# Attention by minima one and two tiles ahead, and small constants turned by TensorE

## The reference

```python
s_loc = jnp.einsum('bjqhd,bkjwhd->bhjqkw', qr, kb).astype(jnp.float32) * scale
s_loc = jnp.where(mask, s_loc + bias.astype(jnp.float32)[None], -jnp.inf)
s_ctx = jnp.einsum('bjqhd,bchd->bhjqc', qr, kc).astype(jnp.float32) * scale
p = jax.nn.softmax(jnp.concatenate([s_loc, s_ctx], axis=-1), axis=-1)
```

## Time and profile before

| | |
|---|---|
| runs | 3012.37 us median of 3 (3010.71 to 3012.51) |
| profiled execution | 3007.67 us, span 3005.7 us |
| busy share of the span | PE 92%, DVE 60%, ACT 41%, POOL 16% |
| start and first group | 0 to 129 us |
| groups 1 to 8 | 129 to 530 us, PE busy 401 of 401 us |
| Fourier phase | 530 to 685 us |
| attention | 685 to 1140 us |
| mixing output, feed-forward | 1140 to 3005 us, PE busy 1758 of 1865 us |

### The profile page before, as it was taken

One profiled execution on the slowest core, in us unless ns is written; L12 is line 12 of the kernel. 1 busy time (PEld: TensorE's weight loads), 2 busy tenths in 40 slices (PEclk: granted clock), 3 DMA queues, 4 the chain that ended last, 5 costly groups with the idle time before them and its releaser, 6 DMA issues. The chain is left out here.

```text
span 3005.7 us, 49988 instructions
## 1 busy us (share of the span) xinstructions
PE 2753.7 (92%) x17010; PEld 2486.7 (83%) x17010; DVE 1788.5 (60%) x3028; ACT 1240.7 (41%) x2612; POOL 466.2 (16%) x670
## 2 busy tenths in 40 slices
PE   4899999766999996998799999999999979999996
PEld 4899999655777785876799999999999968888875
DVE  3533432155999993776777876667666633452445
ACT  2111111125888881322555565556555532122121
POOL 0000000043444330224010000000000000320312
PEclk7999999878999997999899999999999989999998
DMA  8223231498576544463655555544444444334243
GB/s 277 85 85 113 85 95 61 154 361 176 116 146 129 124 80 134 157 203 106 192 167 171 166 192 167 160 153 149 153 151 151 128 154 154 96 129 145 74 129 133
DMA packets 409340, 435.70 MB, mean 145 GB/s; under 512 B 131260, under 2 KB 302286, under 8 KB 406480
## 3 DMA queue, kind: packets, MB, share of 16 engines
q1 hardware_dynamic: 384400, 417.32, 46.5%
q10 hardware_dynamic: 23168, 10.38, 1.2%
q0 software_dynamic: 1600, 5.77, 0.5%
HBM read 311.18 MB, written 124.57 MB: 145 GB/s over the span
## 5 line engine op out<-in xcount | busy, mean ns | idle before, releaser
L2132 PE MATMUL fu_alpha<-fu_h,fu_w 128*128 128x384 f32 x3168 | 574.5, 336 | 19.8 <-DVE fu_h L2358 10.6
L2132 PEld LDWEIGHTS fu_alpha<-fu_h,fu_w 128*128 128x128 f32 x3168 | 553.5, 189 | 22.3 <-issue 22.2
L2618 PE MATMUL fd_acc<-fd_w,fd_f 128*128 128x512 f32 x2376 | 546.5, 392 | 27.4 <-DVE fd_w L2646 18.0
L2618 PEld LDWEIGHTS fd_acc<-fd_w,fd_f 128*128 128x128 f32 x2376 | 447.8, 189 | 126.0 <-issue 18.4
L2132 PE MATMUL fu_beta<-fu_h,fu_w 128*128 128x384 f32 x1584 | 285.4, 334 | 0.6 <-DVE fu_h L2358 0.6
L2132 PEld LDWEIGHTS fu_beta<-fu_h,fu_w 128*128 128x128 f32 x1584 | 275.4, 188 | 1.1 <-issue 1.1
L579 PE MATMUL pj_gps<-pj_ht,w_in 128*128 128x256 f32 x2160 | 270.1, 285 | 0.0
L579 PEld LDWEIGHTS pj_gps<-pj_ht,w_in 128*128 128x128 f32 x2160 | 264.8, 192 | 1.3
L2642 DVE TENSOR_TENSOR fd_f<-fd_f_stage,fd_f 128x512 fp32r<-128x512 f32 (+1 forms) x110 | 91.2, 831 | 284.6 <-ACT fd_f L2598 284.6
L2598 ACT CAST fd_f<-fd_f_stage 128x512 fp32r<-128x512 f32 (+1 forms) x110 | 63.6, 581 | 443.3 <-PE fd_acc L2618 400.8
L2332 DVE TENSOR_TENSOR fu_w<-up_w_stage,fu_w 128x512 fp32r<-128x512 f32 x264 | 181.7, 689 | 84.7 <-ACT fu_w L2196 82.9
(11 more groups left out here) (213 smaller groups left out, 4165.9 us busy)
## 6 DMA issues: line engine op xcount, KB each, us to landing
up_w_stage<-in_w_gu_dram SPq DMA_DIRECT2D x88, 512.0 KB, 4.2
fu_w_sums<-w_gu_sums SPq DMA_DIRECT2D x132, 256.0 KB, 2.9
fd_w_stage<-in_w_down_dram SPq DMA_DIRECT2D x54, 512.0 KB, 3.7
fd_f_stage<-f_t SPq DMA_DIRECT2D x88, 256.0 KB, 2.7
at_k<-k_t SPq DMA_DIRECT2D x28, 704.0 KB, 12.6
w_gu_sums<-fu_w_sums SPq DMA_DIRECT2D x66, 256.0 KB, 5.0
fo_w<-in_w_ada_dram SPq DMA_DIRECT2D x8, 2048.0 KB, 15.0
up_w_stage<-in_w_gu_dram SPq DMA_DIRECT2D x44, 256.0 KB, 4.5
```

The lines of the kernel that those rows point to most:

```text
L2132: mm = pe.matmul(out, w[x][:, j, k, :], b[y][:, j, k, :], start=opens and (k, x, y) == (0, HI, HI), stop=(k, x, y) == (KH - 1, LO, HI), sk ...
L2618: mm = pe.matmul(acc[:, t, at], f[a][:, slot, t * P:(t + 1) * P], w[b][:, w_at(st, slot), at], start=is_step(st, 0) and (a, b) == (HI, HI) ...
```

## The change

In the projection the conditioning vectors, `b_ada` and `a_bs` are loaded as 36 rows of 128 (`small`), turned by one TensorE transpose, and read from PSUM. In group 0 ACT and DVE take the blocks of `w_in` in several pieces between their other work, and `norm_x(2)` comes after the last one. In the attention the queries are scaled by -1/8 and the bias is negated, so a minimum is sought in place of a maximum. The context minimum of a tile is the starting value of the local minimum, which makes the combining instruction needless. Exponentials are taken with scale -1, one tile ahead of the turns; scores and minima are made two tiles ahead, between the turn of the local and of the context part. Row sums have four slots in place of three.

```diff
+        small = zbt[0:ROWS, 0, P:2 * P]
+        turned_small = abps[:, 0, 0:ROWS]
...
-                with nc.allow_non_contiguous_dma(reason="conditioning vectors, channel on partition"):
-                    for v in (LAT, CTX):
-                        sp.dma_start(cond[:, v, :], conds[v].rearrange("(k p) -> p k", p=P)).then_inc(cond_loaded, 16)
+                sp.dma_start(small[COND_ROW:BIAS_ROW, :], conds.rearrange("v (k p) -> (v k) p", p=P)).then_inc(small_loaded, 16)
...
-                    if next2:
+                    first_group = isinstance(g, int) and g == 0
+                    if next2 and not first_group:
                         row_rstd(g + 2)
                     gate_rstd(g * NT + 1)
+                    if first_group:
+                        row_rstd(g + 2)
...
+                act.dma_start(small[BIAS_ROW:BS_ROW, :], b_ada[0, 0:2 * D].rearrange("(k p) -> k p", p=P)).then_inc(small_loaded, 16)
+                act.dma_start(small[BS_ROW:ROWS, :], a_bs.rearrange("l h p -> (l h) p")).then_inc(small_loaded, 16)
                 act.dma_start(zbt[:, 0, 0:P], dft_c64).then_inc(consts_loaded, 16)
                 act.dma_start(zbt[:, 1, 0:P], dft_s64).then_inc(consts_loaded, 16)
                 act.dma_start(ws[:, :, :].rearrange("p a (b q) -> p (a b) q", q=P), a_ws.rearrange("l h p q -> p (l h) q")).then_inc(fw_loaded, 16)
+                act.wait_ge(silu_zeroed, 1)
+                act.wait_ge(small_turned, 1)
+                act.activation(silu[:, :, 0:2].rearrange("p k v -> p v k"),
+                               turned_small[:, COND_ROW:BIAS_ROW].rearrange("p (v k) -> p v k", v=2), ACT.Silu).then_inc(silu_done, 1)
...
                 act.wait_ge(fw_zeroed, 1)
                 for g in range(4):
                     pair, half = g // 2, g % 2
                     act.dma_start(fw2[half * 64:half * 64 + 64, pair * P + half * 64:pair * P + half * 64 + 64],
                                   f_w[0, g]).then_inc(fw_loaded, 16)
-                act.wait_ge(cond_loaded, 32)
-                act.wait_ge(silu_zeroed, 1)
-                act.activation(silu[:, :, 0:2].rearrange("p k v -> p v k"), cond[:, :, :], ACT.Silu).then_inc(silu_done, 1)
-
-                with nc.allow_non_contiguous_dma(reason="biases, channel on partition"):
-                    act.dma_start(mod_bias[:, :], b_ada[0, 0:2 * D].rearrange("(k p) -> p k", p=P)).then_inc(mod_bias_loaded, 16)
-                    act.dma_start(bs[:, :], a_bs.rearrange("l h p -> p (l h)")).then_inc(consts_loaded, 16)
...
                     round_h(0, 0, j)
-                for n in range(3, len(W_BLOCKS)):
-                    high_w(n)
+                high_w(3)
 
                 def group(g, s, next2, next1, is_ctx):
-                    if next1 is not None:
-                        for j in range(SUB):
-                            round_h(g + 1, 1 - s, j, used=g)
                     unit, staged = [0], [0]
+                    first_group = isinstance(g, int) and g == 0
+
+                    def round_next():
+                        if next1 is not None:
+                            for j in range(SUB):
+                                round_h(g + 1, 1 - s, j, used=g)
+
+                    def first_high(*blocks):
+                        if first_group:
+                            for n in blocks:
+                                high_w(n)
+
+                    if not first_group:
+                        round_next()
...
                     gelu(0)
-                    round_qk(HD ** -0.5)
+                    first_high(4)
+                    if first_group:
+                        round_next()
+                    round_qk(-(HD ** -0.5))
                     n = product()
                     act.wait_ge(ab_done, g * NT + NT)
                     columns = gps[:, n, :].rearrange("p (m t q) -> p (m t) q", m=2, t=NT)
                     if reversed_from(g, 0) is not None:
                         columns = columns[:, :, P - 1::-1]
                     act.copy(zbt[:, :, :].rearrange("p m (t q) -> p (m t) q", q=P), columns).then_inc(slot_read[n], 1)
+                    first_high(5, 6)
                     gelu(1)
-                    round_qk(HD ** -0.5)
+                    round_qk(-(HD ** -0.5))
+                    first_high(7, 8)
                     round_qk()
                     ab_to_stage(0)
...
+                pe.wait_ge(consts_loaded, 16 * N_CONSTS)
+                pe.wait_ge(small_loaded, 48)
+                pe.transpose(turned_small, small[:, :], ident[0:ROWS, 0:ROWS]).then_inc(small_turned, 1)
                 pe.wait_ge(silu_done, 1)
                 for n in range(2):
                     ada_product(n)
-                pe.wait_ge(consts_loaded, 16 * N_CONSTS)
...
+                dve.wait_ge(silu_done, 1)
+                dve.tensor_copy(mod_bias[:, :], turned_small[:, BIAS_ROW:BS_ROW]).then_inc(small_read, 1)
+                dve.tensor_copy(bs[:, :], turned_small[:, BS_ROW:ROWS]).then_inc(small_read, 1)
                 norm_x(0)
-                dve.wait_ge(consts_loaded, 16 * N_CONSTS)
...
-                for n in range(2, 4):
+                for n in range(2, 5):
...
-                    low_qk(0, 1, HD ** -0.5)
-                    if isinstance(g, int) and g == 0:
-                        for n in range(4, len(W_BLOCKS)):
-                            low_w(n)
-                    if next2:
+                    first_group = isinstance(g, int) and g == 0
+
+                    def first_low(*blocks):
+                        if first_group:
+                            for n in blocks:
+                                low_w(n)
+
+                    low_qk(0, 1, -(HD ** -0.5))
+                    first_low(5)
+                    if next2 and not first_group:
                         norm_x(g + 2)
                     gate_norm(1)
-                    low_qk(1, 4, HD ** -0.5)
+                    first_low(6)
+                    low_qk(1, 4, -(HD ** -0.5))
+                    first_low(7, 8)
+                    if first_group:
+                        norm_x(g + 2)
                     gate(0)
...
+        def row_slot(tile):
+
+            return (tile[2] + tile[1] * (TILES % 4)) % 4
...
-                        pool.tensor_tensor(from_cols, rel[:, parity, :, at],
-                                           col_mask[:, c, 0:w].unsqueeze(1).to_broadcast([P, REL_TILE_ROWS, w]), ALU.add).then_inc(cols_done, 1)
+                        pool.tensor_tensor(from_cols, col_mask[:, c, 0:w].unsqueeze(1).to_broadcast([P, REL_TILE_ROWS, w]),
+                                           rel[:, parity, :, at], ALU.subtract).then_inc(cols_done, 1)
...
-                def turn(tile):
+                def turn_local(tile):
...
+                def turn_more(tile):
+                    h, parity, pos = tile
+                    s = pos % 2
+                    u = h * TILES + pos
+                    n = blocks_of(pos)[0]
                     pe.wait_ge(exp_done, u + 3)
                     pe.wait_ge(lo_done, u)
...
-                        qk(after)
-                    turn(tile)
+                    turn_local(tile)
+                    if two_after(tile) is not None:
+                        qk(two_after(tile))
+                    turn_more(tile)
                     if before is not None:
                         pv(before)
...
-                def row_max(tile):
+                def context_min(tile):
+
+                    h, parity, pos = tile
+                    s = pos % 2
+                    n = blocks_of(pos)[0]
+                    if n and pos == FIRST_OF[KIND_OF[pos]]:
+                        dve.wait_ge(bias_ready, h * len(KINDS) + KIND_OF[pos] + 1)
+                    dve.wait_ge(qk_done, h * TILES + pos + 3)
+                    dve.tensor_reduce((cmin if n else nmx)[:, s:s + 1], ctx_ps[:, s, 0:T_PAST if n else T_CTX], AX_X,
+                                      ALU.min).then_inc(cmin_done if n else nmax_done, 1)
+
+                def local_min(tile):
 
                     h, parity, pos = tile
                     s = pos % 2
                     n = blocks_of(pos)[0] * blocks_of(pos)[1]
-                    i = KIND_OF[pos] if n else None
-                    if n and pos == FIRST_OF[i]:
-                        dve.wait_ge(bias_ready, h * len(KINDS) + i + 1)
-                    dve.wait_ge(qk_done, h * TILES + pos + 3)
-                    dve.tensor_reduce(ncmax[:, s:s + 1], ctx_ps[:, s, 0:T_PAST if n else T_CTX], AX_X, ALU.max, negate=True).then_inc(cmax_done if n else nmax_done, 1)
                     if n:
-                        dve.tensor_tensor_reduce(prob[:, s, 0:n], loc_ps[:, s, 0:n], bias[:, BIAS_AT[i]:BIAS_AT[i + 1]], 1.0, 2 * MASKED,
-                                                 ALU.add, ALU.max, lmax[:, s:s + 1]).then_inc(smax_done, 1)
-                        dve.wait_ge(smax_done, h * N_LAT + pos + 1)
```

(91 more changed lines are left out.)

19 lines of the change are left out of this document (8 added, 11 removed).

## The result

The changed kernel takes 3077.04 us, median of 4 runs (3074.18 to 3078.41), the kernel before on the same chip 3011.54 (3009.98 to 3012.51): a ratio of 1.0218, 95% interval 1.0203 to 1.0232. It is 66 us slower where 37 us faster was forecast. The profiled execution has a span of 3074.6 us against 3005.7.

What follows compares the result with a forecast made beforehand. TensorE waits in the first token group (53 of 66 us busy); attention has no engine at its limit. Gains of 12 + 25 = 37 us from 3007.7 give 2970.7; the median, 4.7 higher, is 2975, range 2962 to 2989.

Steps and rivals of the forecast that it cites:

- Start: Projection's start and first token group: constants loaded as rows give 1.5 us, the split weight rounding 10.5; together 12 us.
- The new loop: Attention: with the lookahead a latent tile takes 2.85 us instead of 3.02; attention gains 25 us, bounds 0 and 45.
- closes over two steps: Attention: TensorE's hand-over, turns, product and scores (3.07) plus a DVE step (2.63) span two tiles, 2.85 us each.
- TensorE's sequence alone: Attention: TensorE's own work per tile is about 2.5 us, so it does not decide the pace.
- What goes: Attention: removing L1452, the two-maxima instruction stretched by GpSimd, ends interference of 2.7 us a head for seven heads.
- What is added: Attention: the local instruction's wait for the context minimum costs DVE 0.08 plus about 0.03 us a tile.
- (a): Attention: the loop isn't there and DVE's floor decides, 46.2 us a head, 2954 us in all; chance 0.18.
- (b): Only the start gains; the attention loop stays as long as the disturbed one before, 3000 us; chance 0.17.
- (d): The start does not gain, the blocks' new places making DVE late for the mixing: 2986 us; chance 0.10.
- (c): Attention: the scalar operand lets GpSimd block the local instruction; 3033 us at 0.45 us stretch a tile; chance 0.07.
- if tiles are above 3.0: Attention: a named sign that the forecast is wrong, against latent tiles forecast at 2.85 us in every head.

Runs made afterwards that it cites:

- start alone: The changed kernel's projection with the attention of the kernel before, scores not negated: 2994.87 us, ratio 0.9953.
- two banks: The single-slot control with the product's two slots in two PSUM banks, the product waiting only for its own slot's sum: 2982.58 us, ratio 0.9911.
- sum alone: Changed kernel with DVE's sum first in the step, ahead of the context minimum, and a [128 x 1] copy between the minima: 2971.85 us, ratio 0.9884.
- one-ahead run: Changed kernel with the old lookahead (scores and minima one tile ahead), negated scores and fused local instruction kept, a copy added: 2975.97 us, ratio 0.9891.
- scores first besides: The sum-alone kernel with TensorE's scores of the tile two later also ahead of the local turn: 2970.57 us, ratio 0.9875.
- control with the single slot: Changed kernel with one PSUM slot for the local turned tiles and scores ahead of the local turn on TensorE: 3053.42 us, ratio 1.0147.

## Why the prediction was wrong

**Start, right.** Forecast 12 us, measured 14.6 in the trace and 14 in the run of the start alone, inside the bounds. The load of `x` gave 1.8 of it against 1.5. TensorE was at the mixing at 89 instead of 91.7, without a wait; it stood 1.88 us ahead of the transposes of the second half where 3.87 had been. The mean clock of 63 to 129 rose from 0.87 to 0.97.

**The failed step.** It is "The new loop". It lists TensorE's sequence correctly, and has the context turn waiting for the low part and the context minimum for the scores. It leaves out the product's own wait, for DVE's sum, and so finds only a loop that "closes over two steps". The change moves the sum from behind the low parts of one step to behind the next but one tile's context minimum, and the rule for a moved step (who waits for it, and what does it now stand behind) was not applied to it. Its term of the sum, 25 us gained, came out as 80 us lost between the first and the last context minimum (434.0 us before, 513.9 after). Without that wait the forecast's numbers are met: 2.85 us a tile was said, and the run with two banks has 51.0 us heads with tiles mostly at 2.8 to 2.9; the run with the sum alone moved ends at 2972, where 2975 was forecast for the change as it was made.

**Met in number, not in mechanism.** That a loop over two steps sets 2.85 is not shown, and the agreement is in part luck. The run with the old lookahead doesn't have that loop and takes 2.86 us a tile as well, and it has about 19 of the 23 us by which the sum alone is below the start alone. So most of the gain goes with the small instruction that went, and little with the lookahead. The prediction also put TensorE's sequence alone at "about 2.5" and set it aside, while the four pieces that it lists for TensorE (0.39, 1.09, 0.35, 1.08) add up to 2.91, more than the 2.85 of the loop. By the stretches above TensorE's work is 2.75 a tile, with hardly any idle time between, so TensorE itself is the likelier limit once the wait is gone; a busy share alone doesn't prove it.

**What goes, right.** The interference on L1452 was priced at 2.7 us a head; the one-ahead run, which differs from the start alone in that, in the copy and in the longer local instruction, saves 2.3 (52.95 to 50.64 for head 6). Heads 6 and 7 now take the same for their sixteen tiles, 45.68 and 45.80, where the start alone has 48.24 and 45.64.

**What is added, nearly right.** The wait of DVE on itself costs what was said, 0.12 against 0.11: 0.73 from the context minimum's start to the next instruction's (905.33 to 906.06), where the start alone has 0.61 for the same 0.69 us long instruction (906.16 to 906.77). But the local instruction itself became longer: 608 against 545 ns at 384 columns, 508 against 444 at 288, 742 against 681 at 512, so 0.06 us a tile that the sum hadn't.

**Rivals.** (a), (b) and (d) are out as totals. (c), the other side, got the sign and not the mechanism: the local instruction with its scalar operand lies between 507 and 752 ns in all 128 tiles, and within 0.01 us of one value for each of the three widths, so GpSimd does not stretch it. By the Trainium skill, SBUF — State Buffer, "Who interferes with whom", a DVE instruction with one SBUF input, outside the 2-port perf modes, does not contend with GpSimd; the trace agrees and adds that a per-row scalar does not count as the second. The true loss was in no rival: each of them kept the order of DVE's step and asked only for its length. The signs that were named did point to it: "if tiles are above 3.0".

**Open.** The jumps of the unrolled loop, in heads 3 and 5, cost 5.4 to 5.7 us in the changed kernel, 4.0 to 4.5 before, 3 with the start alone, 3.4 with the sum alone moved and 5.3 with the scores first besides. Nothing here explains that spread. It wasn't tried what the best kernel takes without its copy, nor what loop paces the control with the single slot in its parts.

## What to carry to other kernels

When a step is moved in one engine's queue, list for each instruction in it every semaphore that it raises, and for each of those what waits, and look up the count it waits for: a wait "for the slot" can be for the *other* slot when two slots share a PSUM bank. Then write out each cycle of waits and over how many tiles it closes; one that closes over a single tile can be the pace however idle the engines are, as here. A reader of results that are overdue goes first in its engine's step, ahead of anything that has to wait, and a small instruction with two SBUF inputs beside a busy GpSimd should be priced by its mean, not by its shortest.

## What the runs showed of the hardware

The fused sum and minimum that begins from a column in SBUF takes 0.06 us longer than the fused sum and maximum that begins from a constant (608 against 545 ns, 742 against 681), whatever the width; no run has the minimum with a constant, so column and minimum are not told apart. It is not stretched by GpSimd. A DVE copy of [128 x 1] isn't either (153 to 155 ns in 127 of them), while the two-input instruction of the same size goes from 159 up to 1173 ns in heads 0 to 6 and stays at 160 in head 7, where GpSimd builds no bias. A reduction of 512 columns lets the next DVE instruction start 0.60 us after its own start, and 0.72 when that one waits for its result (medians over the 128 tiles of the kernel before and of the one-ahead run).
